# Two transformer blocks: the FFN's up projections as seven block products in place of eight, and the residual in memory during the FFN

## The reference

```python
    mixed = jnp.concatenate([y_att, y_conv, y_ssd], axis=-1) @ w_out[l]
    x = x + rms_norm(mixed, norm_mix_post[l])
    h = rms_norm(x, norm_ffn_pre[l])
    u = causal_dwconv(h @ ffn_w_up[l], ffn_conv_w[l]) + ffn_conv_b[l]
    gate, up = jnp.split(u, 2, axis=-1)
    x = x + rms_norm((jax.nn.silu(gate) * up) @ ffn_w_down[l], norm_ffn_post[l])
```

## Time and profile before

| | us |
|---|---|
| runs | 2310.32, 2310.47 (median), 2311.59 |
| traced execution, first to last instruction (span) | 2307.0 |
| median beyond that span | 3.5 |
| PE busy | 2228.0 (97%) |
| DVE busy | 1170.0 (51%) |
| POOL busy | 1019.7 (44%) |
| ACT busy | 716.6 (31%) |
| matmuls | 9862 |

### The profile page before, as it was taken

The page is one execution under the profiler, slowest core; times in us unless marked ns, Lnnn a source line. Parts: engine busy times, 40 slices in busy tenths (PEclk is TensorE's granted clock), DMA queues, the critical chain, the costliest instruction groups (busy, mean ns, idle before and its releaser), DMA issues.

```text
span 2307.0 us, 27430 instructions
## 1 busy us (share of the span) xinstructions
PE 2228.0 (97%) x9862; PEld 1728.0 (75%) x9862; DVE 1170.0 (51%) x1240; ACT 716.6 (31%) x1132; POOL 1019.7 (44%) x821
## 2 busy tenths in 40 slices
PE   7999999999899999999999988999999999999998
PEld 5777755577688888888887766777767777788887
DVE  6864355546654433333333878666665556411223
ACT  4243256633311111111112344555344334200112
POOL 3533410176644444444444663232235653444475
PEclk9999999999999999999999999999999999999999
DMA  5111100132211111111111231000101111111153
GB/s 205 50 37 37 37 10 10 38 127 73 66 53 45 53 47 45 52 48 45 46 54 46 76 131 44 28 27 27 37 28 37 54 36 37 46 51 49 45 164 119
DMA packets 34031, 130.61 MB, mean 57 GB/s; under 512 B 4132, under 2 KB 4516, under 8 KB 33196
## 3 DMA queue, kind: packets, MB, share of 16 engines
q1 hardware_dynamic: 30960, 111.39, 15.1%
q10 hardware_dynamic: 3004, 18.30, 2.1%
HBM read 117.04 MB, written 12.58 MB: 56 GB/s over the span
## 4 chain that ended last, share of the span: by engine, by line
PE 84%; DVE 4%; ACT 4%; issue 4%; POOL 2%; DMA 1%; SPq 0%; ACTq 0%; POOLq 0%; DVEq 0%
PE PG L671 14%; PE PG L677 13%; PE PG L676 13%; PE PG L1219 5%; PE PG L1225 5%; PE PG L1224 5%; PE PG L1026 2%; PE PO L1290 1%; PE PO L1048 1%; PE PT L1040 1%; PE PG L730 1%; DMA WR<-weights 1%; PE PG L736 1%; PE PG L735 1%; POOL WH L564 1%
## 5 line engine op out<-in xcount | busy, mean ns | idle before, releaser
L564 POOL TENSOR_TENSOR WH<-WR,zero 128x512 fp32r<-128x512 f32 x380 | 417.2, 1098 | 1182.4 <-PE PG L671 666.9
L567 POOL TENSOR_TENSOR WL<-WR,WH 128x512 fp32r<-128x512 f32 x380 | 541.0, 1424 | 29.8
L671 PE MATMUL PG<-HH,WH 128*128 128x512 f32 x1136 | 450.0, 396 | 2.0 <-POOL WL L567 1.2
L677 PE MATMUL PG<-HH,WL 128*128 128x512 f32 x1136 | 443.4, 390 | 0.0
L676 PE MATMUL PG<-HL,WH 128*128 128x512 f32 x1136 | 443.2, 390 | 0.0
L671 PEld LDWEIGHTS PG<-HH,WH 128*128 128x128 f32 x1136 | 213.8, 188 | 51.1 <-issue 4.5
L676 PEld LDWEIGHTS PG<-HL,WH 128*128 128x128 f32 x1136 | 213.7, 188 | 46.1 <-issue 2.4
L677 PEld LDWEIGHTS PG<-HH,WL 128*128 128x128 f32 x1136 | 213.8, 188 | 44.9
L1219 PE MATMUL PG<-HH,WH 128*128 128x512 f32 x544 | 226.0, 415 | 5.6 <-ACTq L2074 2.7
L1225 PE MATMUL PG<-HH,WL 128*128 128x512 f32 x544 | 213.1, 392 | 0.0
L1224 PE MATMUL PG<-HL,WH 128*128 128x512 f32 x544 | 212.3, 390 | 0.0
(11 more groups left out here) (542 smaller groups left out, 4134.2 us busy)
## 6 DMA issues: line engine op xcount, KB each, us to landing
WR<-weights SPq DMA_DIRECT2D x196, 512.0 KB, 3.5
RAW<-x SPq DMA_DIRECT2D x8, 512.0 KB, 7.7
x_spill<-X ACTq DMA_DIRECT2D x1, 4096.0 KB, 12.6
X<-x_spill ACTq DMA_DIRECT2D x1, 4096.0 KB, 13.0
x_spill<-X ACTq DMA_DIRECT2D x4, 1024.0 KB, 5.4
X<-x_spill ACTq DMA_DIRECT2D x8, 512.0 KB, 4.0
y<-RAW SPq DMA_DIRECT2D x7, 512.0 KB, 5.0
POSI<-positions ACTq DMA_DIRECT2D x1, 512.0 KB, 15.2
```

The costliest lines, as they stand in the source:

```text
L564: pool.tensor_tensor(WH[:, slot, part], WR[:, slot, part], zero[:, :].to_broadcast([P, HALF]), ALU.add).then_inc(w_hi, 1)
L567: pool.tensor_tensor(WL[:, slot, part], WR[:, slot, part], WH[:, slot, part].bitcast(F32), ALU.subtract).then_inc(w_split, 1)
L671: m = pe.matmul(out[:, cut], WH[:, slot, w], hi[:, cut], start=n == 0, stop=False)
L677: m = pe.matmul(out[:, cut], WL[:, slot, w], hi[:, cut], start=False, stop=last)
```

## The change

The up projections of 19 of the 22 tiles are computed by Strassen's scheme (in the form with fewer additions). The 2x2 block matrices are: weights, gate and up columns by the upper and lower half of the 1024 channels; input, upper and lower half of the channels by left and right half of the positions. Seven products of 4 weight blocks against 512 positions, 12 matmuls each, replace eight.

- The input's sums and differences are made once, on VectorE, in X's own place (`form_sum`), with their high parts by ScalarE (`form_high`) and low parts by VectorE (`form_low`), during the new third tile `ffn_next`, which is still computed the old way. X goes to memory before (`put_away`, six transfers from ScalarE's queue) and comes back in the last tile. The norms of j = 0, 1 are written over X, and wait for those transfers.
- The weights' sums and differences are made by GpSimd for each tile (`combine`, 4 a tile), in `WR`. The high parts `WH` of the loop's weights are made by ScalarE (`high`), the low parts by GpSimd (`low`). Both work on parts of 512, in a ring of four buffers.
- Of the seven products two go on adding in a bank; ScalarE copies two banks out, and VectorE makes five additions, into `CG` and `CU`, from which the convolution's taps are then computed (ScalarE the last weight and bias, VectorE the other two), no longer from PSUM.
- VectorE, not ScalarE, makes `GH`. SiLU is written to `PRD`. RAW isn't set to zero; the first turn copies.
- A turn of the loop is now: down projection, tile A, tile B.
- Eight semaphores that only marked one event each are one (`dve_mark`), with the same waits.

```diff
+        PRODUCTS = ((0, True), (1, True), (2, True), (3, True), (0, False), (3, True), (2, False))
+        RAW_PARTS = ((0, 0), (0, 0), (1, 0), (0, 0), (0, 1), (1, 1), (0, 1))
+        SUMS_MADE = {1: 1, 2: 2, 3: 3, 6: 4}
...
+            def banks(self):
+                if self.second:
+                    return [PG[:, n // 2, halves(n)] for n in range(4)]
+                return [PT[:, 0, :], PT[:, 1, :], PO[:, 0, :], PO[:, 1, :]]
...
@@ SyncE
+            with sp.Fori(0, TURNS) as i:
+                for n, (done, s) in enumerate(((2, 0), (4, 1), (10, 1), (11, 0), (17, 0), (18, 1))):
+                    sp.wait_ge(u_lo, PARTS * i + done)
+                    load_at(6 * i + (FFN_RAW + 2 + n), s)
...
@@ GpSimd
+            def block_sums(b):
+                lows(0)
+                b.loaded(pool, 1)
+                combine(1, upper_1, upper_1, lower_1, ALU.subtract, 1)
+                combine(2, lower_1, lower_1, lower_2, ALU.add, 1)
+                lows(1)
+                combine(3, upper_1, lower_2, upper_1, ALU.subtract, 2)
+                lows(2)
+                lows(3)
+                lows(4)
+                combine(4, upper_2, upper_2, upper_1, ALU.subtract, 5)
+                lows(5)
+                lows(6)
...
+            block_sums(tail)
+            for q in range(2):
+                pool.wait_ge(u_done, tail.product(4 + q))
+                split_part(FFN_RAW // 2, 0, q)
+            pool.wait_ge(u_done, tail.product(6))
+            split(FFN_RAW // 2, 1)
...
@@ TensorE
+            def block_products(b):
+                banks = b.banks()
+                for k, (bank, fresh) in enumerate(PRODUCTS):
+                    pe.wait_ge(u_lo, b.part(k))
+                    if k in FORMS_MADE:
+                        pe.wait_ge(c_lo, 2 * KT + FORMS_MADE[k])
+                    if k == 4:
+                        primed(pe, c_copy, b.copied(1))
+                    if k in (5, 6):
+                        primed(pe, c_add, b.added((1, 3)[k - 5]))
...
-            with pe.Fori(0, FFN_PAIRS - 2) as i:
-                g = Groups("ffn", i, 8)
-                gate_up(g, 0, 0, i, 6)
-                down(down_banks(i), 2, i, i, 6)
-                gate_up(g, 6, 4, i, 6)
-            for x in range(2):
-                gate_up(Groups("ffn_tail"), 2 * x, 2 * x, stage="ffn_tail")
+            gate_up(Groups("ffn_next"), 0, 0, stage="ffn_next")
+            with pe.Fori(0, TURNS) as i:
+                down(down_banks(i), i)
...
+                block_products(Blocks(i))
...
+                block_products(Blocks(i, 1))
+            block_products(Blocks(0, tail=True))
             last_downs()
...
@@ ScalarE
+            def high_block(b, k):
+                if k == 0:
+                    b.loaded(act, 0)
+                if k in SUMS_MADE:
+                    act.wait_ge(u_sum, b.summed(SUMS_MADE[k]))
+                if k >= 4:
+                    act.wait_ge(u_done, b.product(k - 4))
+                high(k, b.raw(k))
...
+            def block_tile(b, follow):
+                first_copy(b)
+                for k in (4, 5, 6):
+                    high_block(b, k)
+                second_copy(b)
+                if follow is not None:
+                    after_block(b, 0, follow)
+                block_tap(b, 1)
+                if follow is not None:
+                    for k in (1, 2, 3):
+                        after_block(b, k, follow)
+                block_tap(b, 0)
+                block_silu(b)
...
             for k in range(KT):
                 chain_square(1, k)
+                if k % 2:
+                    put_away(1, k - 1, k + 1)
...
@@ VectorE
             def chain_norm(j, k, vname):
                 cut = halves(j)
                 dve.wait_ge(c_x, KT * (j + 1))
-                if k >= 2:
-                    dve.wait_ge(c_lo, KT * j + (k - 1))
+                if j < 2:
+                    dve.wait_ge(x_away, 32 + 64 * j)
+                elif k >= 2:
+                    dve.wait_ge(c_lo, chain_tiles(j) + (k - 1))
...
+            def block_tile(b):
...
+                add(1, b.product(3), CG[:, RIGHT_HALF], CG[:, LEFT_HALF], banks[3])
+                add(2, b.product(1), CU[:, LEFT_HALF], CG[:, RIGHT_HALF], banks[1])
+                add(3, b.product(2), CU[:, RIGHT_HALF], CU[:, LEFT_HALF], banks[2])
+                add(4, b.product(5), CU[:, LEFT_HALF], CU[:, LEFT_HALF], banks[3])
+                dve.wait_ge(f_act, b.twice_tile(1))
+                step(tap(1, 1))
+                add(5, b.product(6), CG[:, RIGHT_HALF], CG[:, RIGHT_HALF], banks[2])
+                tap(1, 2).then_inc(f_taps, 1)
+                dve.wait_ge(f_act, b.twice_tile(2))
+                step(tap(0, 1))
+                tap(0, 2).then_inc(f_taps, 1)
+                product(b.tile(1))
...
+            def turn_tiles(i, first=False):
+                accumulate(down_banks(i), first)
+                split_product(2 * i + 3, 0)
+                block_tile(Blocks(i))
+                split_product(2 * i + 4, 1)
+                block_tile(Blocks(i, 1))
```

More of the change, by code:

```diff
@@ L48 @@
 STAGE_GROUPS = [("x", TT), ("in", 18), ("kv", 8), ("mla", MLA_GROUPS * 4),
[L49 removed]
+                ("out", 2 * KT), ("ffn_first", 2), ("ffn_next", 2), ("ffn", 4 * (FFN_PAIRS - 2)),
                 ("ffn_last", 2 * KT), ("diff", 3),
@@ new lines, in _, with turn_tiles @@
+            form_high(3, XR[:, LOWER, LEFT_HALF], X[:, LOWER, RIGHT_HALF])
+            def turn_tiles(i, follow):
+                banks, first, second = down_banks(i), Blocks(i), Blocks(i, 1)
+                for k in range(4):
+                    bank, n = banks(2 * k + 1)
+                    bank.ready(act, n)
+                    high_block(first, k)
+                block_tile(first, lambda k: high_block(second, k))
+                block_tile(second, follow)
+            with act.Fori(0, TURNS - 1) as i:
+                turn_tiles(i, lambda k: high_down(k, i + 1))
```

432 lines of the change are left out of this document (311 added, 121 removed).

## The result

The changed kernel takes 2319.69 us (median of 5 runs, 2317.99 to 2321.96) against 2310.47 us before in the same runs (2308.22 to 2311.59): ratio 1.0042, 95% interval 1.0029 to 1.0055. It is slower by 9.2 us, where 5.0 slower was forecast. The change removed 51.7 us of matmuls, and TensorE loses all of that and more in waits and at half clock.

A forecast was written before the change was run, and what follows sets the result against it. TensorE's matmuls were taken to bound the kernel before (busy 97%). Savings of 57.4 us against added stalls of 63.0 summed to +5.6 us; the forecast was 2310.5 + 5 = 2315.5 us, range 2286 to 2333.

The forecast's parts named there:

- B2: Third product of a loop turn's second tile: TensorE 0.4 us late, waiting for GpSimd's low part.
- B4: Second tile's fifth product: high part queued behind SiLU, low part 2.4 us late, 0.4 of it already at B2.
- B5: Second tile's sixth product: low part behind GpSimd's fourth sum, meeting VectorE's cast and subtraction, 1.2 us late.
- fifth down tile: In each turn, waits for the first accumulation, which VectorE reaches only after the second tile's taps and product: 0.7 us.
- signs that I named: TensorE waiting for WL at second tile's fifth, sixth products and ffn_last; tap and low-part means well above 1.28, 1.30; turns about 64.3.
- The first (another phase of the two engines): Faster rival: VectorE and GpSimd hold each other less in the loop; 2264 us without holds; 2262 to 2304, chance 0.20.
- The second (the port as the bound from a turn of 65.2 us up): Slower rival: VectorE and GpSimd excluding each other bounds the loop; 2328 to 2334 us; chance 0.25, alone or with clock.
- The third (the clock): Rival: TensorE at half speed after waits in the last tile, about 3 us, 2319 us; no separate chance.
- the last tile: Its products follow the second tile without downs between, so loads, sums and low parts lack slack: 3.1 + 1.9 + 1.2 = +6.2 us.
- A0: First turn's first low part, 2.5 us late behind VectorE's sums and low parts of the input; part of +4.1 net.
- Old waits: Waits of the kernel before, from ffn_first's last 24 matmuls to ffn_last's 48th, given back or replaced: -5.7 us.
- First splits of ffn_last: GpSimd starts late and alternates with VectorE's last seven operations: 4.0 + 3.0 + 1.9 + 2.3 = +11.1 us; X's return +1.

The follow-up runs named there:

- e3: Changed kernel, VectorE's four taps of each turn's first tile reading PSUM instead of SBUF (other values): 2302.8 us, ratio 0.9974, a turn 62.46 us.
- e1: Changed kernel, ScalarE making the second tile's fifth and sixth high parts and first bank copy ahead of SiLU, likewise the last tile: 2332.5 us, ratio 1.0096.
- e5: Changed kernel, ScalarE's high parts ahead of SiLU and VectorE's second-tile additions ahead of the first tile's product and cast: 2286.5 us, ratio 0.9905.
- e7: Changed kernel, only VectorE's order edited: second-tile additions ahead of the first tile's product and cast: 2316.4 us, ratio 1.0028, a turn 63.79 us.
- e10: Changed kernel, high parts of the loop's weights made by GpSimd again instead of ScalarE: 2371.6 us, ratio 1.0267, a turn 69.79 us.
- e2: Changed kernel, the transfers bringing X back issued behind the last tile's SiLU instead of ahead of its taps: 2316.6 us, ratio 1.0036.
- e11: Changed kernel, the six transfers putting X away carrying 32 of each 512 columns (other values): 2321.0 us, ratio 1.0048.
- e12: Changed kernel with both engines' orders edited, last tile's additions moved, X back later, and first-tile taps reading PSUM (other values): 2279.6 us, ratio 0.9870.

## Why the prediction was right, and where its numbers were off

**The mechanism was right.** Its stalls in the loop, from the rows of the turn at 910 to 974 us (a start's distance to the one before, less 0.227):

| | forecast us | measured us |
|---|---|---|
| B2 | 0.4 | 0.5 |
| B4 | 2.0 | 1.7 |
| B5 | 1.2 | 1.1 |
| fifth down tile | 0.7 | 0.3 |
| first down part | 0.2 | 0.1 |
| second matmul after each wait (0.34 apart) | none | 0.5 |
| a turn | 64.3 | 64.24 |

That the taps are held is shown by e3, that B4's high part waits in ScalarE's queue by e1 and e5 beside e7. By e3 the rule of the Trainium skill (SBUF — State Buffer, section "SBUF: two separate sides") agrees with the runs: the same tap with one input in PSUM takes 1282 ns and holds nobody (the low part beside it, at 942.91 in e3, takes 1.29 us, and 2.01 at 951.70 after the change). Of the signs that I named, the up taps' mean of 1362 ns is hardly above 1.28; the gate taps carry it. The sum had no term for the restart: behind each wait a further 0.11 us goes, five times a turn. B4 and the fifth down tile, which I set too high, made up for it.

**The rivals.** The first (another phase of the two engines) didn't come up: the eight turns behind the first are alike within 0.4 us. Its arithmetic was tested in part by e3: without the taps' holds it had 2282 us for both tiles; for one of the two tiles 2302.8 were measured. The second (the port as the bound from a turn of 65.2 us up) didn't decide, but e10 shows that it takes some 18 more operations of GpSimd a turn to get near it. The third (the clock) came, in three places of the FFN in the traced run: behind waits of 2.37 and 2.75 us in the first turn and the last tile, and at ffn_last's first splits. The first of them, timeline and window:

```profile
676.37 0.50 PE L1321 MATMUL PT<-T3H,WH 128*128 128x512 f32 x1 [2.37 <-POOL WL L691]
```

```profile
676.30:681.00 4.70, 4.63 (x13) 3.68 (x14) 0.00 (x0) 1.63 (x3) 4.54 (x5) 0.64 0.00 0
```

A granted clock of 0.64 there is half speed for some ten matmuls, about 2 us.

That the totals of the first turn and of the last tile fit is luck in part. In the first turn A0 came 1.0 us late and not 2.5, and the clock took 2 us that my sum didn't hold. In the last tile TensorE was 0.1, 2.9 and 1.1 us late where I had 6.2 in all, and some 1.8 us of half clock filled the gap.

**Where 5.0 became 9.2.** The sum was 5.6 us, and the 5 in the forecast drops 0.6 of it without a reason. Between the two spans it is 11.5 us (2318.5 and 2307.0), twice the sum. The median before lies 3.5 us beyond its traced span, after 1.2, and I had taken 3.5 for both. Wherever the record has a run's time beside its own span, they are 1.8 to 2.1 us apart; so the rest of these 3.5 and 1.2 tells which execution was traced, a faster one than the median before and a slower one after. That part of the nearness of 5.0 and 9.2 is luck as well. The sizes below are between the traced executions: 3.0 of the 5.9 us that the sum lacks have come up to the 25th matmul of ffn_last, the others behind it.
- Old waits. I took the 48th matmul of ffn_last before to end at 1261.86 + 10.9 = 1272.7. But 1261.86 is not the first of the 48: the stage starts at 1257.67 and the 25th matmul at 1266.02, so the 48th ends at 1271.5. The waits given back were 4.4 us and not 5.7: 1.3 us.

```profile
1257.67 0.39 PE L1154 MATMUL PG<-GH,WH 128*128 128x512 f32 x1
...
1266.02 0.39 PE L1154 MATMUL PG<-GH_LAST,WH 128*128 128x512 f32 x1
```

- ffn_next took 22.6 us for 21.8 of matmuls, the first turn 69.0 for 68.4: 1.4 us. The last tile took 25.1 for 25.2. Turns 2 to 9 were 1.0 us shorter than eight times 64.35.
- First splits of ffn_last: 18.5 us from the last product's end (1256.08) to 1274.61, 17.5 forecast. The parts were mis-sized: X's return delayed the load by 5.1 us (e2), where I had 1. The alternation then cost less than my 11.1, since VectorE's last operations were partly over when the late load came. Half clock (0.50 on the mean of 1260.9 to 1271.2) is in the 18.5 us too and was not in my sum.
- Before the FFN, costed at nothing: 0.7 us (e11). I looked at the transfers' way, which was hidden as forecast, and not at where the normalised tile now lies.
- GpSimd's own time was taken at 1.25 us an operation, where the row has 1.30: 33.8 us a turn and not 32.5, which changes nothing.
- Behind ffn_last, where the order is as before, the traced run had 0.7 us more at the next norm, and 1.6 in the differential mixer, where the same wait of 1.97 us was followed by a clock of 0.72 on the mean of 6 us, and of 1.00 before. I can't say whether the change has a part in it; no run here tells.

**Range and chances.** The time lies inside the likeliest case's own range (2304 to 2324) and on its side. What I didn't see is how near the fast version was: the places of a few instructions on two engines make 33 us.

## What to carry to other kernels

When work is moved to idle engines, their shares of busy time say little; walk one period through each engine's list, and for every wait ask what stands behind the waiting instruction. Where two queues are late by nearly the same amount, mending one shows nothing or makes it worse, so look at both before an order is judged. Where GpSimd works beside it, an input of VectorE's that stays in PSUM is worth more than its own duration shows, as long as what it would hold is on the way to TensorE: 1.8 us a turn in e3, 0.66 in e12.
